# Two LayerNorms of a streaming encoder: squares of the distance from an early shift, taken beside the tiles that make r

## What is computed

```
def layer_norm(x, g, b):
    mu = jnp.mean(xf, axis=-1, keepdims=True)
    var = jnp.mean(jnp.square(xf - mu), axis=-1, keepdims=True)
    return ((xf - mu) * lax.rsqrt(var + LN_EPS) * g + b).astype(x.dtype)
...
        x = layer_norm(ALPHA * x + y, g[1], b[1])
        x = layer_norm(ALPHA * x + 0.5 * swiglu(x, w['ffn_w_in'][l, 1], w['ffn_w_out'][l, 1]), g[2], b[2])
```

## Time and profile before

| | us |
|---|---|
| median of 3 runs | 2372.91 (2372.08 to 2373.29) |
| the profiled execution | 2374.91 |
| its span in the profile | 2373.0 |
| TensorE matmul busy | 2286.6 (96%) |
| VectorE busy | 1525.6 (64%) |
| ScalarE busy | 1157.8 (49%) |
| GpSimd busy | 583.4 (25%) |
| granted TensorE clock, mean | 0.982 |

### The profile page before, as it was taken

One profiled execution on the slowest core, in us unless ns is written; L12 is line 12 of the kernel. 1 busy time (PEld: TensorE's weight loads), 2 busy tenths in 40 slices (PEclk: granted clock), 3 DMA queues, 4 the chain that ended last, 5 costly groups with the idle time before them and its releaser, 6 DMA issues. The chain is left out here.

```text
span 2373.0 us, 42348 instructions
## 1 busy us (share of the span) xinstructions
PE 2286.6 (96%) x17003; PEld 2244.4 (95%) x17003; DVE 1525.6 (64%) x2302; ACT 1157.8 (49%) x1947; POOL 583.4 (25%) x499
## 2 busy tenths in 40 slices
PE   8999999999998999999999999999999999899997
PEld 8989999999998898999999999999999999889997
DVE  6887768556787677444474566655677666465444
ACT  4445543555643556433354455655466554354332
POOL 2256501123310343111251123011252011132110
PEclk9999999999998999999999999999999999999999
DMA  9667675454675454654569655544556446345552
GB/s 234 171 182 221 188 213 184 120 168 134 191 223 156 125 172 142 187 151 145 147 179 292 181 160 172 154 124 135 149 152 183 132 146 187 109 146 161 146 151 82
DMA packets 702292, 391.11 MB, mean 165 GB/s; under 512 B 25001, under 2 KB 689042, under 8 KB 702098
## 3 DMA queue, kind: packets, MB, share of 16 engines
q1 hardware_dynamic: 662720, 332.44, 49.0%
q10 hardware_dynamic: 39378, 55.96, 7.1%
HBM read 366.53 MB, written 21.82 MB: 164 GB/s over the span
## 5 line engine op out<-in xcount | busy, mean ns | idle before, releaser
L468 DVE TENSOR_TENSOR wl<-raw,wh 128x1024 fp32r<-128x1024 f32 (+1 forms) x640 | 792.9, 1239 | 481.4 <-ACT wh L462 479.7
L484 PE MATMUL tile_ps<-xh,wh 128*128 128x256 f32 (+1 forms) x3520 | 1066.0, 303 | 25.6 <-DVE wl L468 13.0
L485 PE MATMUL tile_ps<-xl,wh 128*128 128x256 f32 (+1 forms) x3520 | 1048.3, 298 | 0.0
L486 PE MATMUL tile_ps<-xh,wl 128*128 128x256 f32 (+1 forms) x3520 | 1047.9, 298 | 0.0
L462 ACT CAST wh<-raw 128x1024 fp32r<-128x1024 f32 (+1 forms) x640 | 656.3, 1026 | 770.6 <-PE tile_ps L486 746.9
L484 PEld LDWEIGHTS tile_ps<-xh,wh 128*128 128x128 f32 x3520 | 674.1, 192 | 35.8 <-DVE wl L468 17.8
L485 PEld LDWEIGHTS tile_ps<-xl,wh 128*128 128x128 f32 x3520 | 675.4, 192 | 1.1 <-issue 0.2
L486 PEld LDWEIGHTS tile_ps<-xh,wl 128*128 128x128 f32 x3520 | 674.6, 192 | 0.0
L594 POOL TENSOR_TENSOR hl<-hf,hh 128x256 fp32r<-128x256 f32 (+1 forms) x176 | 252.5, 1435 | 1300.5 <-ACT hh L526 1300.0
L484 PE MATMUL tile_ps<-hh,wh 128*128 128x320 f32 (+1 forms) x1472 | 446.3, 303 | 19.5 <-POOL hl L594 18.7
L486 PE MATMUL tile_ps<-hh,wl 128*128 128x320 f32 (+1 forms) x1472 | 435.8, 296 | 0.0
(11 more groups left out here) (293 smaller groups left out, 1774.3 us busy)
## 6 DMA issues: line engine op xcount, KB each, us to landing
raw<-in_ffn_w_in_dram SPq DMA_DIRECT2D x352, 512.0 KB, 3.9
raw<-in_ffn_w_out_dram SPq DMA_DIRECT2D x128, 448.0 KB, 3.7
raw<-in_ffn_w_out_dram SPq DMA_DIRECT2D x64, 512.0 KB, 4.1
raw<-in_ssm_w_glu_dram SPq DMA_DIRECT2D x32, 512.0 KB, 3.9
raw<-in_attn_w_kv_dram SPq DMA_DIRECT2D x32, 512.0 KB, 3.9
wt<-scr_w ACTq DMA_DIRECT2D x16, 512.0 KB, 4.2
cp<-scr_c ACTq DMA_DIRECT2D x16, 512.0 KB, 3.7
raw<-in_attn_w_q_dram SPq DMA_DIRECT2D x16, 512.0 KB, 4.1
```

The costliest lines, as they stand in the source:

```text
L468: nc.vector.tensor_tensor(wl[n % WS][:, 0:k, :], raw[n % RAWS][:, 0:k, :], wh[n % WS][:, 0:k, :].bitcast(F32), ALU.subtract).then_inc(w_lo, 1)
L484: nc.tensor.matmul(o, wh[w][:, kk, :], xa, start=kk == 0, stop=False)
L485: nc.tensor.matmul(o, wh[w][:, kk, :], xb, start=False, stop=False)
L486: mm = nc.tensor.matmul(o, wl[w][:, kk, :], xa, start=False, stop=kk == ROWS[n] - 1)
```

## The change

For the norms in `QUICK` the squares are no longer taken of r less its mean. After the first two blocks of r exist, TensorE sums them over partitions; ScalarE makes of this a shift, their mean over 256 features. For each block d, as soon as it exists, VectorE writes r less the shift into a scratch tile (`sq` or `zq`), ScalarE squares that in place, and TensorE adds it into a PSUM bank. This runs as steps of the tiles that make r (16 GLU tiles, 8 o tiles), by the tables `Q_SHIFT`, `Q_DIST`, `Q_SQ`, `Q_SUM`. After out tile 0 TensorE adds `zc`, `r[7]` and the last two squares; ScalarE makes the mean; VectorE computes the variance from mean, shift and sum of squares in four dependent instructions. Centring then follows in pairs with the scaling, blocks 0 to 4 on VectorE and 5 to 7 on GpSimd.

```
-            dve.wait_ge(ln_mean, e + 1)
-            for d in range(DT):
-                V.tensor_tensor(r[:, d, CS[h]], r[:, d, CS[h]], cb[:, 0:N], ALU.subtract).then_inc(ln_cent, 1)
-                if d == 3:
-                    yield
...
+        Q_SHIFT = (5, 3)
+        Q_DIST = ((6, 6, 7, 8, 9, 11, 13, 15), (3, 3, 4, 4, 5, 5, 6, 7))
+        Q_SQ = ((7, 7, 8, 9, 10, 12, 14, 15), (4, 4, 5, 5, 6, 6, 7, 7))
+        Q_SUM = ((9, 9, 10, 11, 12, 14, 16, 16), (5, 5, 6, 6, 7, 7, 8, 8))
+        Q_NEXT = (16, 8)
+        Q_DVE = 5
...
+            nc.tensor.matmul(misc[:, 1, 0:N], ones[:], zc[:, 0:N], start=True, stop=True).then_inc(ln_sh, 1)
...
+            A.activation(cb[:, 0:N], misc[:, 1, 0:N], ACT.Copy, scale=1.0 / (2 * P)).then_inc(ln_shift, 1)
...
+                V.tensor_tensor(sqq[d % 4][:, 0:N], r[:, d, CS[h]], cb[:, 0:N], ALU.subtract).then_inc(ln_cent, 1)
+            yield from idle(Q_NEXT[q] - at)
             dve.wait_ge(ln_mean, e + 1)
...
+            link(dve, V.tensor_tensor(cb[:, 0:N], rstd[:, 0:N], cb[:, 0:N], ALU.subtract))
+            link(dve, V.tensor_tensor(cb[:, 0:N], cb[:, 0:N], cb[:, 0:N], ALU.mult))
+            dve.wait_ge(ln_mm2, e + 1)
+            link(dve, V.scalar_tensor_tensor(out=cb[:, 0:N], in0=misc[:, 2, 0:N], scalar=1.0 / D, in1=cb[:, 0:N],
+                                             op0=ALU.mult, op1=ALU.subtract))
+            V.tensor_scalar(cb[:, 0:N], cb[:, 0:N], 0.0, None, ALU.max).then_inc(ln_var, 1)
+            centre(0)
+            centre(1)
+            dve.wait_ge(ln_sd, e + 1)
+            V.reciprocal(cb[:, 0:N], cb[:, 0:N]).then_inc(ln_rstd, 1)
+            dve.wait_ge(ln_rstd, e + 1)
+            scale(0)
+            scale(1)
+            yield
+            centre(2)
+            scale(2)
+            centre(3)
+            scale(3)
+            yield
+            centre(4)
+            scale(4)
+            scale(5)
+            yield
+            scale(6)
+            scale(7)
+            yield
+
+        def pool_ln_quick(pool, ln, h, split):
+            e, N = LN_TURN[ln, h], NT[h]
+            yield
+            pool.wait_ge(ln_sd, e + 1)
+            after_halves(pool)
+            for d in range(Q_DVE, DT):
+                nc.gpsimd.tensor_tensor(r[:, d, CS[h]], r[:, d, CS[h]], rstd[:, 0:N], ALU.subtract).then_inc(ln_qp, 1)
             yield from idle(2)
             for d in range(DT):
                 pool.wait_ge(ln_out, 8 * e + d + 1)
                 pool_lo(pool, h, d, split)
-                if d in (1, 3, 5):
+                if d in (0, 2, 4, 6):
                     yield
             yield
```

More of the change, by code:

```diff
@@ L566, in dve_add @@
                                                op0=ALU.mult, op1=ALU.add).then_inc(drained[n % PSS], 1)
+                if last_first and d == DT - 1:
+                    step(beside)
                 dve_lo(dve, n + WS)
-                step(beside)
+                if not (last_first and d == DT - 1):
+                    step(beside)
         halves_issued, hl_issued, sums_issued, squares_issued, lows_issued = [0], [0], [0], [0], [0, 0]
@@ L745, in pool_lo @@
                                     ALU.subtract).then_inc(x_ready[h], 1)
-        sqq = sq + [zq]
[L751 to L758, removed]
-            for d in range(DT):
+        ln_sh = sem("ln_shift_sum")
@@ new lines, in pe_ln_quick @@
+        def pe_ln_quick(pe, ln, h):
+            e, N, q = LN_TURN[ln, h], NT[h], QUICK.index((ln, h))
+            yield from idle(Q_SHIFT[q])
+            pe.wait_ge(ln_zc, ZC_AT[ln, h] + 1)
+            nc.tensor.matmul(misc[:, 1, 0:N], ones[:], zc[:, 0:N], start=True, stop=True).then_inc(ln_sh, 1)
+            at = Q_SHIFT[q]
+            for d in range(DT):
+                yield from idle(Q_SUM[q][d] - at)
+                at = Q_SUM[q][d]
+                if d == DT - 2:
+                    pe.wait_ge(ln_zc, ZC_AT[ln, h] + 6)
+                    nc.tensor.matmul(misc[:, 3, 0:N], ones[:], zc[:, 0:N], start=True, stop=False)
+                    pe.wait_ge(*made(ln, h, DT - 1))
+                    nc.tensor.matmul(misc[:, 3, 0:N], ones[:], r[:, DT - 1, CS[h]], start=False, stop=True
+                                     ).then_inc(ln_mm1, 1)
@@ L760, in pe_ln_quick @@
                 pe.wait_ge(ln_sq, 8 * e + d + 1)
[L761 to L763 removed]
+                mm = nc.tensor.matmul(misc[:, 2, 0:N], ones[:], sqq[d % 4][:, 0:N], start=d == 0, stop=d == DT - 1)
                 mm.then_inc(ln_mm2 if d == DT - 1 else ln_acc, 1)
[L765 to L767 removed]
@@ L800, in dve_ln_quick, with centre @@
             e, N, V = LN_TURN[ln, h], NT[h], nc.vector
-            dve.wait_ge(ln_mean, e + 1)
-            for d in range(DT):
-                V.tensor_tensor(r[:, d, CS[h]], r[:, d, CS[h]], cb[:, 0:N], ALU.subtract).then_inc(ln_cent, 1)
-                if d == 3:
-                    yield
-            yield from idle(2)
+            q = QUICK.index((ln, h))
+            def centre(d):
+                V.tensor_tensor(r[:, d, CS[h]], r[:, d, CS[h]], rstd[:, 0:N], ALU.subtract).then_inc(ln_qd, 1)
@@ new lines, in scale @@
+            def scale(d):
+                if d < Q_DVE:
+                    dve.wait_ge(ln_qd, Q_DVE * q + d + 1)
+                else:
+                    dve.wait_ge(ln_qp, (DT - Q_DVE) * q + d - Q_DVE + 1)
+                V.tensor_tensor(r[:, d, CS[h]], r[:, d, CS[h]], cb[:, 0:N], ALU.mult).then_inc(ln_mul, 1)
+            at = 0
+            for d in range(DT):
+                yield from idle(Q_DIST[q][d] - at)
+                at = Q_DIST[q][d]
+                if d == 0:
+                    dve.wait_ge(ln_shift, q + 1)
+                if d >= 4:
+                    dve.wait_ge(ln_acc, 7 * q + d - 3)
+                dve.wait_ge(*made(ln, h, d))
+                V.tensor_tensor(sqq[d % 4][:, 0:N], r[:, d, CS[h]], cb[:, 0:N], ALU.subtract).then_inc(ln_cent, 1)
@@ L2498, in _ @@
             finish(beside)
-            act_glu(act, 0)
             beside = act_ln_quick(act, 1, 0)
+            act_glu(act, 0, beside)
             act_out(act, 0, 1, 2, beside)
```

67 lines of the change are left out of this document (35 added, 32 removed).

## The result

The changed kernel takes 2381.0 us (median of 8 runs, 2378.6 to 2381.5), the kernel before on the same chip 2373.1; the two medians lie 7.9 us apart. The ratio of the runs is 1.0027, with an interval of 1.0018 to 1.0036, which is worth 6.4 us, 4.3 to 8.5. The profiled execution took 2380.27 us, its span is 2378.4, its mean granted clock 0.982.

A forecast was written before the change was run, and what follows sets the result against it. TensorE, busy for 96% of the span, was taken as the bound, with GpSimd's queue setting the first in tile at each norm. Norm (1, 0) +2.0 and norm (4, 1) +4.1 gave +6.1 us: 2372.9 to 2379.0, range 2369 to 2386.

The forecast's parts named there:

- The main line: Both norms: losses at the turn and in VectorE's and GpSimd's queues exceed the early root's gain; 5 to 9 us lost; chance 0.45.
- Turn: Z, when TensorE turns from out tile 0 to matmuls with ones, comes 2.4 and 2.9 us later at the two norms.
- The early root: ScalarE's root ends at Z+6.2 at norm (1, 0), 7.6 us earlier, and at Z+6.1 at norm (4, 1).
- Turns of the two engines: Four VectorE centre and scale instructions alternate with GpSimd's centrings: 0.95 us each at norm (1, 0), 1.15 at (4, 1).
- the +8 of the prediction: Strict port rule, VectorE and GpSimd excluding each other for whole instructions: a pair about 1.1 us, total +8 instead of +6.
- Late `wl`: TensorE waits for `wl`: 1.8 us before tile 21 at norm (1, 0); 1.2, 3.4, 0.8, 1.0 at norm (4, 1).
- GpSimd's line: GpSimd's queue of sums and `xl` ends at Z+33.8 and Z+35.0, setting the end of the first in tile.
- The clock: Low granted clock after TensorE's wait, around the first in tile: taken as unchanged.
- the rival: Clock falls inside the out tiles, around the 3.4 us wait before tile 13: 5 us at most, 2384; chance 0.12.
- Port cheap: VectorE and GpSimd at both norms: disturbed pair below about 0.6 us, first in tile near Z+26, 2360; chance 0.12.
- half price: VectorE and GpSimd overlap more: a pair 0.75 us, a `wl` 0.7, about +3, 2376, no change; chance 0.26.
- A table step too early: Blocked VectorE holds up a `wl` ahead of Z: one or two tiles at 1 to 2 us, 2385; chance 0.05.

The follow-up runs named there:

- experiment 1: The change at one norm only, against the kernel before: norm (1, 0) alone -0.9 us by the runs, norm (4, 1) alone +7.1 us.
- after_again: The changed kernel, unchanged, run for a second trace; +6.4 us (3.8 to 9.3) by the runs against the kernel before.
- only_second: The change at norm (4, 1) alone, norm (1, 0) as in the kernel before; 2381.0 us, +7.1 us by the runs.
- fast_after: The changed kernel with squares written as fp32r and summed in one pass; -1.7 us by the runs against the kernel before.
- late_after: The changed kernel with GpSimd's sums of blocks 5 to 7 for the next norm behind the last `xl`; ratio 0.9995 to the kernel before.
- late_fast_after: The changed kernel with both fp32r sums of squares and the next norm's sums behind the last `xl`; ratio 0.9973 to the kernel before.
- centre_dve: The changed kernel with the centring of blocks 5 to 7 moved from GpSimd to VectorE; +4.0 us by the runs against the kernel before.
- no_pool_centre: The changed kernel with GpSimd's centring of blocks 5 to 7 left out; -0.5 us by the runs against the kernel before.
- experiment 2: Both kernels run again unchanged: the kernel before 2374.1 us (2374.7 beside it), the changed kernel +6.4 us by the runs against the kernel before.

## Why the prediction was right, and the term that was too small

The forecast was 2379.0 us, +6.1; the median is 2381.0, the ratio worth +6.4, and the marks have +6.7. The main line held: the norm's early root is won, and more than that is lost at the turn and in the line of VectorE and GpSimd. That the numbers agree so well is in part luck, for two errors of opposite sign stand in the sum, and what the marks do not see came to -0.3 us here, but to -2.7 and +2.5 us with one norm alone (experiment 1).

- **Turn.** Predicted 2.4 and 2.9 us late; it is 2.98 and 3.68. This is the mis-sized term. "Two cost 0.68 and four 1.53" was read from the start of the first matmul with ones to the start of the tile matmul behind. But that one starts early and lasts long: 0.50 us instead of 0.31. Its end, less 0.31, gives 0.87 for two, 0.43 each; at 320 columns 0.52 + 2088.03 - 0.28 - 2087.20 = 1.07 for two (0.28 is a tile matmul of 256 columns), 0.53 each. Seven are 3.0 and 3.7. The rows had the right price.
- **The early root.** Predicted to end at Z+6.2 and 6.1; it ends at Z+6.4 and 6.3.
- **Turns of the two engines.** Predicted 0.95 and 1.15 us for each of four VectorE instructions beside GpSimd; measured a mean of 0.94 and 1.07. An instruction that takes 0.48 us alone (0.41 from start to start), and an `xl` of 0.83, would make 1.24 to 1.31 at 320 columns if they shut each other out for their whole length. That is the rule of the Trainium skill ("SBUF — State Buffer", SBUF: two separate sides) weighed above. 1.07 is less: the rule would have given too much, the +8 of the prediction against 6.7.
- **Late `wl`.** Predicted 1.8 us before tile 21; 1.2, 3.4, 0.8 and 1.0 at norm (4, 1). Measured 1.30; 1.06, 2.78 and none for the last two.
- **GpSimd's line.** Predicted to end its last `xl` at Z+33.8 and 35.0; it ended at Z+32.9 and 34.2. Hence behind the turn 0.9 us were won at norm (1, 0), where I had 0.4, and 0.96 lost at norm (4, 1), where I had 1.2. These errors, 0.5 and 0.2 us too dear, cancel about half of the 1.4 us by which the turn was too cheap.
- **The clock.** Taken as unchanged. It was not. The 4 us from Z+16 at norm (4, 1), in before and in after (busy us of PE, PEld, DVE, ACT, POOL, then granted clock, DMA share, GB/s):

```profile
2103.20:2107.20 4.00, 4.00 (x37) 4.00 (x36) 3.30 (x5) 2.47 (x4) 1.48 (x2) 1.00 0.27 69
```

```profile
2106.74:2110.74 4.00, 3.68 (x17) 3.69 (x18) 3.97 (x7) 2.40 (x5) 2.31 (x2) 0.50 0.44 131
```

  So the clock did fall to its 1.2 GHz level among the out tiles, at the 2.78 us wait for `wl` that ends at 2107.06, as the rival said. The same stretch has 0.61 in after_again, 0.60 in only_second and 0.50 in fast_after and late_after, all with that wait, but 1.00 in late_fast_after, which has it too, and 1.00 in centre_dve and no_pool_centre, where the waits for `wl` are shorter. What the rival had wrong is the price. GpSimd's line ended later anyway: in after the clock is back at 1.00 only from Z+24, in after_again from Z+20, and the first in tile ends at 35.48 and 35.46. In the 4 us behind it (Z+36) the clock is 0.55 in after, 0.97 in after_again and 0.93 in before; that goes with the 1.5 us of experiment 2, where the rival had up to 5.
- **The rivals.** Port cheap, and half price: a pair took 0.94 and 1.07 us, against under 0.6 and 0.75 in these rivals, so both are out. A table step too early: seven matmuls of 0.43 us make 3.0, and the turn is 2.98 us late, so no step of the tables holds up a weight ahead of it.

## What to carry to other kernels

Work moved ahead of a critical point isn't free because the engines that prepare it are idle there: its matmuls run on the engine that sets the time, and are paid in full. When two engines slow each other, moving work between them gains little; drop it, make it cheaper, or put behind the critical line what no one needs yet. And where a change is worth a few us of 2374, read marks in the trace that surround it beside the median, and report where the two disagree: the marks repeat to hundredths but see only their stretch.

## What the runs showed that was not expected

- Two traces of one program stand up to 2.9 us (before) and 5.7 us (after) apart in between, in whole stretches: TensorE busy 20 of 20 us with a granted clock of 0.89 or 0.98. The sums over the program partly cancel.
- Each of three edits to the changed kernel (no centring on GpSimd, cheap sums of squares, late sums) takes 6.9 to 8.1 us off by the runs, as much as the whole loss, but 3.1 to 5.2 us by the marks. Why was not found.
- A matmul of fp32 costs 0.43 us at 256 and 0.54 us at 320 columns from start to start, one of fp32r 0.15 us at 320. The tile matmul behind an fp32 one is recorded with 0.50 us instead of 0.31, as if its start were noted some 0.2 us early.
